# Small triangular inversions on 32x32 tiles of the tensor engine instead of 64x64 ones

## The chip, the cores and the metric

The kernel runs on 1 core of one Trainium2 chip. The metric is the device time of one execution in microseconds (us). The kernel before took 3010.54 us, the median of 3 runs (3006.62 to 3010.95).

## The reference

Three transformer-like blocks run one after the other on 512 tokens of width 1024, all in float32. Two of them hold a recurrence that is computed in chunks, and each chunk needs the inverse of a unit lower triangular matrix:

- the gated delta rule of block 1 (8 heads, chunks of 64 tokens in the reference; the kernel takes 128). Cut to its core:

```
amat = where(strict, kk * decay * beta, 0)          # per head and chunk, strictly lower
t = triangular_solve(eye + amat, rhs, lower=True, unit_diagonal=True)
```

- the RWKV-7 recurrence of block 2 (8 heads), which the reference runs token by token and the kernel in chunks of 64 tokens, again with an inverse of a unit triangular matrix per head and chunk.

Everything else (projections, feed-forward parts, norms, attention with a top-k mask, convolutions) is dense products and elementwise work; the change does not touch it.

## The kernel before

All matrices lie with 128 partitions. Of the projection products ("dense" steps, lines 1063 to 1065) each is three products of a 128x128 weight with a 128x512 operand in a rounded float32 format; they are most of the tensor engine's work.

**The order.** One list gives, for every engine, the order of its steps. In the stages with recurrences the list is made by a planner, `weave`: it takes chains of small dependent steps (one chain per group of heads) and a supply of dense tiles, simulates the engines with a table of costs per step (`SEG`, lines 297 to 312: `p`, `v`, `s`, `g` are the tensor, vector, scalar and GpSimd engines) and writes down the order in which it would issue them. So a changed cost in the table moves steps of all engines. Every engine works strictly through its own list, and steps wait for each other by semaphores. On the tensor engine dense tiles fill the time between small steps.

**The inversions.** There are 12: 8 for the heads of the delta rule (kind `g`, four chunks of 128 tokens each side by side in a 128x512 tile) and 4 for pairs of heads of RWKV-7 (kind `r`, eight chunks of 64 tokens for two heads: two rows of eight 64x64 blocks, in a 128x512 tile). The strictly triangular matrix is first masked to its 16x16 diagonal blocks. Their inverse is the product (I - D)(I + D^2)(I + D^4)(I + D^8), so in three levels the kernel squares D and its transpose (tiles `d` and `e`) and updates the partial product `p`:

- `il` (line 1245), levels 0 and 1: two products, d'e into one bank and e'd into another; level 2: one. The scalar engine copies one bank to `e` (line 2700), the vector engine the other to `d` (line 1955).
- `ip` (line 1257), three levels: e'p into a third bank.
- `ipv` (line 1957), three levels: the vector engine adds that bank to `p`, 128x512 at a time (line 1960).

Then the blocks of 16 are joined to blocks of 32, 64 (and, for kind g, 128) by the steps `it` (transpose of p), `im`, `in_`, `iu` and masked copies made by GpSimd (`iq`).

**How a product is issued.** The products of `il` and `ip`, and those of `im` and `in_`, go through `product(v)`, which is `blocks64` (kind g, lines 1105 to 1112: the 64x64 blocks on the diagonal, 8 matmuls) or `halves64` (kind r, lines 1114 to 1121: 16 matmuls). Each is a float32 matmul of 64 rows by 64 columns with 64 columns moving, on two diagonal 64x64 tiles of the array in turn. A float32 matmul with a small operand stands in the trace as two records of MATMUL and two of LDWEIGHTS. `turned` (line 1128) transposes on the same two tiles, `corner` (line 1237) multiplies 64x64 blocks off the diagonal, and `rt` and `rm` of kind r (transposes and 64x64 products for the recurrence) are woven between the steps of the inversion.

In numbers: each inversion has 5 products in `il` and 3 in `ip`, so 8 products of 16-blocks: 64 for kind g and 32 for kind r.

Of the kernel before, what the change touches and what calls it, by code (L numbers as in the profile page):

```python
# [14 lines left out]
MUL, ADD, SUB, MAX, MIN = ALU.mult, ALU.add, ALU.subtract, ALU.max, ALU.min  # L15
# [148 lines left out]
    return ap.rearrange("p (t i) -> p t i", t=4)  # L164


def v8(ap):
    return ap.rearrange("p (t i) -> p t i", t=8)

# [120 lines left out]
def IXN(qb, h):  # L290
# [7 lines left out]
    dense="p1.36", sums="p.32 v2.0 s.69", xd="p.43 v.68", bt="p.43 s.6", cb="p.86 v.68", st0="v1.7", st="p.86 v1.14",  # L298
    ch="p.23 v.68", che="s2.1", cm="v.75|g1.3", sz="s.6 v.69", sy="p1.6 v1.6", sn1="s.63", sn1p="p.25", sn2="v2.7", sn2p="p.45", sn3="v.74",
    pair="s.63 v.75", hq="p.86", hqs="s1.2", hn="v6.9", hnp="p.43", hn2="s.6", hg="p.23 v1.38 s1.23", hb="p.23 v1.5",  # L300
    eq="p.43 s.6", ek="p.43 s.6", ea="v1.6", eb="v3.2", ec="v1.0", ep="p.43 s.6", hu="p1.72 v1.38", i0="g1.3|p.43 s.6 v1.5", il="p1.0 s.6|v.69", il2="p.5 s.6", iu="p.5 s.6", ip="p.5", ipv="v.69", it="p.5 s.6", iq="g1.28", im="p.5 v.69",
    in_="p.5 v.65", hk="p.5 v2.0", hs1="p.22 v.35", hs2="p.22 s.28", hs3="p.54 v.33", ho="s.36", hon="v4.0",
    hos="p.43", ho2="v.74", hz="s.6 v.69", conv="s.72 v2.24", conv2="s.63 v.75", gate="s.6", branch="v.7", part="v1.4", sh="s.69 v.74", wd="s.63",
    ru="p1.2 s1.37", r1="v2.3 s.63", r1p="p.2", r2="v2.6", r2p="p1.72", r3="v2.3", r3p="p.86", r3b="v1.38", r4="v4.4|s1.9",
    ra="p1.9 s.6 v2.1", ril="p1.9 s.6|v.69", ril2="p.95 s.6", riu="p.95 s.6", rip="p.95", rit="p.95 s.6", rim="p.95 v.69", rin_="p.95 v.65",
    rm="p.95 v.69", rt="p.95 s.6", s1="p.25 s.27", s2="p.13 v.4", s4="p.25 v.2", s3="p.36", ry1a="s.6",
    ry1="p.86 v.69", ry2a="s.62", ry2="p.2", ry2n="v2.6", ry3p="p1.72", ry3="v3.0", rg="s.63", ixp="s.6", ixw="p.05 v.2",
    ixs="p.64 s.5 v.6", ixt="v1.2", ax="s.6", ap="s.6", av="p.43 s.6", an0="p.86", an1="s1.18", an2="v5.2", an2p="p.43",
# [7 lines left out]
def seg(s):  # L316

    kind = s[0]
    if kind == "il" and s[1] == 2:
        kind = "il2"  # L320
    if s[0] in ("il", "ip", "it", "im", "in_", "iu") and s[-2] == "r":
        kind = "r" + kind
    return SEG[kind]
# [11 lines left out]
def opens(name, j):  # L335
# [27 lines left out]
    "ipv": lambda n, *v: [("ip", n) + v],  # L363
    "it": lambda *v: [("ipv", 2) + v], "iq": lambda n, *v: [("im", n - 1) + v if n else ("il", 2) + v],
    "im": lambda n, *v: [("iq", n) + v] * (n < 2) + [("in_", n - 1) + v if n else ("ipv", 2) + v],
# [260 lines left out]
def inversion(v, levels):  # L626
    out = [("i0",) + v]
    for lev in range(3):
        out += [("il", lev) + v, ("ip", lev) + v, ("ipv", lev) + v]
    out += [("iq", 0) + v, ("it",) + v]  # L630
    for n in range(levels):
        out += [("im", n) + v] + ([("iu", n - 1) + v] if n else []) + ([("iq", n + 1) + v] if n + 1 < min(levels, 2) else []) + [("in_", n) + v]
    return out
# [10 lines left out]
def rwkv_pair(p):  # L644
    out = [("ru", p), ("r1", p), ("r1p", p), ("r2", p), ("r2p", p), ("r3", p), ("r3p", p), ("r3b", p), ("r4", p),
           ("ra", p), ("rt", p, 0)]
    v = ("r", p)
    for lev in range(3):
        out += [("il", lev) + v, ("ip", lev) + v, ("ipv", lev) + v] + ([("rt", p, lev + 1)] if lev < 2 else [])
# [247 lines left out]
def build(nc, D, out):  # L897
    with ExitStack() as stack:
# [23 lines left out]
        def t(i):  # L922
            return tile[i]
# [115 lines left out]
        def tensor(e, w):  # L1039
# [83 lines left out]
            def turned(b, x, compact):  # L1123

                for c in range(8):
                    for k in (0, 64) if compact else (64 * (c % 2),):
                        g, s = slice(k, k + 64), slice(c * 64, c * 64 + 64)
                        i = e.matmul(b[g, s], x[g, s], C("ident")[g, g], start=True, stop=True)  # L1128
                return i

            def product(v):
                return halves64 if v[0] == "r" else blocks64

# [111 lines left out]
            def il(lev, *v):  # L1245
                V_ = INV[v]
                w.wait_ge(*IV.dve.at("p0", v) if lev == 0 else IV.dve.at("d", v, lev - 1))
                if lev:
                    w.wait_ge(*IV.act.at("e", v, lev - 1))
                elif v[0] == "r":  # L1250
                    w.wait_ge(*RW.act.at("tok", v[1], 0))
                i = product(v)(bank[V_.bx], t(V_.d), t(V_.e))
                if lev < 2:
                    i = product(v)(bank[V_.bz], t(V_.e), t(V_.d))
                i.then_inc(*IV.pe.up("sq", v, lev))

            def ip(lev, *v):
                V_ = INV[v]
                w.wait_ge(*IV.act.at("e", v, lev))
                w.wait_ge(*(IV.dve.at("p", v, lev - 1) if lev else IV.dve.at("p0", v)))  # L1260
                if lev and v[0] == "r":
                    w.wait_ge(*RW.act.at("tok", v[1], lev))
                product(v)(bank[V_.by], t(V_.e), t(V_.p)).then_inc(*IV.pe.up("p", v, lev))

            def it(*v):
                V_ = INV[v]
                w.wait_ge(*IV.dve.at("p", v, 2))
                turned(bank[V_.bx], t(V_.p), v[0] == "r").then_inc(*IV.pe.up("pt", v))

            def im(n, *v):  # L1270
                V_ = INV[v]
                if n < 2:
                    w.wait_ge(*IV.pool.at("q", v, n))
                w.wait_ge(*(IV.dve.at("m", v, n - 1) if n else IV.dve.at("p", v, 2)))
                i = corner(bank[V_.bz], t(V_.L), t(V_.p), 64) if n == 2 else product(v)(bank[V_.bz], t(V_.d), t(V_.p))
                i.then_inc(*IV.pe.up("y", v, n))

# [358 lines left out]
        def vector(e, w):  # L1636
# [320 lines left out]
            def ipv(lev, *v):  # L1957
                V_ = INV[v]
                w.wait_ge(*IV.pe.at("p", v, lev))
                e.tensor_tensor(t(V_.p), t(V_.p), bank[V_.by], ADD).then_inc(*IV.dve.up("p", v, lev))  # L1960

            def im(n, *v):
                V_ = INV[v]
# [583 lines left out]
            def fc4(h):  # L2547
# [5 lines left out]

            do = dict(acc=acc, rms2=rms2, rms=rms, h=h, xg=xg, xscale=xscale, pair=pair, ffg=ffg, ffs=ffs, ffu=ffu, res=res,
                      conv=conv, conv2=conv2, sums=sums, xd=xd, st0=st0, st=st, ch=ch, cb=cb, cm=cm, sz=sz, sy=sy, sn2=sn2,
                      sn3=sn3, i0=i0, il=il, ipv=ipv, im=im, in_=in_, ea=ea, eb=eb, ec=ec, hn=hn, hg=hg, hb=hb, hu=hu, hk=hk, hs1=hs1, hs3=hs3,
                      hon=hon, ho2=ho2, hz=hz, part=part, branch=branch, ada0=ada0, ada=ada, ada3=ada3, halves=halves,
                      ixw=ixw, ixs=ixs, ixt=ixt, sh=sh, r1=r1, r2=r2, r3=r3, r3b=r3b, r4=r4, ra=ra, rm=rm, s2=s2, s4=s4, ry1=ry1,
                      ry2n=ry2n, ry3=ry3, an2=an2, sa=sa, sb=sb, dg=dg, do_=do_, gv=gv, gw=gw, gn=gn, gnn=gnn, gn2=gn2, gs=gs,
# [656 lines left out]
```

## Time and profile before

| | |
|---|---|
| median of 3 runs | 3010.54 us |
| the profiled execution itself | 3006.34 us |
| its span (first to last instruction) | 3004.6 us |
| tensor engine busy | 2925.2 us, 97% |
| vector engine busy | 1531.4 us, 51% |
| scalar engine busy | 1062.9 us, 35% |
| GpSimd busy | 1375.9 us, 46% |
| mean granted clock of the tensor engine | 0.989 |

A busy tensor engine is one with at least one matmul under way; matmuls overlap in the array, so that the time of one record (218 ns for a 64x64 one) is not what it costs. What a step costs on the chain is the distance from its start to the next one's. The inversions of kind g lie between 265 and 670 us, those of kind r between 1190 and 1245 us and between 1410 and 1465 us.

### The profile page before, as it was taken

The page shows a single profiled execution, that of the slowest core. Times are in us where ns is not written, and L with a number is a line of the kernel's source. Part 1 is how long each engine was busy: PE and PEld are TensorE (multiplying, and loading weights), DVE is VectorE, ACT ScalarE, POOL GpSimd, SP SyncE. Part 2 cuts the span into 40 slices and gives each one's busy share as a digit, 9 for nine tenths or more (in the row PEclk, how much of TensorE's full clock was granted, in tenths as well). Part 3 has the DMA queues.
Part 4 walks back from the last instruction along what each step waited for, and adds up shares of the span by engine and source line. Part 5 has one row for each costly group of instructions (what it writes and reads, how often), then busy time and mean ns, then how long its engine had stood idle before and what let it go on. Part 6 is the DMA issues. An engine that isn't in the chain of part 4 may idle for free.

```text
span 3004.6 us, 45720 instructions
## 1 busy us (share of the span) xinstructions
PE 2925.2 (97%) x18672; PEld 2364.3 (79%) x18672; DVE 1531.4 (51%) x3042; ACT 1062.9 (35%) x1760; POOL 1375.9 (46%) x1781
## 2 busy tenths in 40 slices
PE   6999999999999999999999999999999999999999
PEld 5778888877888887857877788888877778888887
DVE  5776567575666416459543543333375773333310
ACT  4453333333322223233234433222454554332221
POOL 4555334345556553124244365555443334545553
PEclk9999999999999999979999999999999999999999
DMA  3212212112444431102022223333322112233332
GB/s 124 84 57 68 68 56 69 58 49 88 125 148 147 125 101 61 31 30 77 24 67 88 64 85 98 94 94 109 99 77 64 57 57 92 91 94 96 98 104 86
DMA packets 72081, 247.99 MB, mean 83 GB/s; under 512 B 8128, under 2 KB 8512, under 8 KB 71744
## 3 DMA queue, kind: packets, MB, share of 16 engines
q1 hardware_dynamic: 71872, 245.08, 26.6%
q8 instruction: 147, 2.41, 0.3%
q14 instruction: 62, 0.51, 0.1%
HBM read 242.95 MB, written 2.10 MB: 82 GB/s over the span
## 4 chain that ended last, share of the span: by engine, by line
PE 88%; DVE 9%; ACT 2%; issue 1%; POOL 0%; DMA 0%; SPq 0%; DVEq 0%; ACTq 0%
PE bank L1063 25%; PE bank L1065 24%; PE bank L1064 24%; PE bank L1120 2%; PE bank L1111 2%; PE bank L1097 2%; PE bank L1563 1%; PE bank L1074 1%; PE bank L1128 1%; PE bank L1581 1%; PE bank L1404 1%; PE bank L1572 1%; PE bank L1103 1%; DVE sm L1655 0%; DVE t L1716 0%
## 5 line engine op out<-in xcount | busy, mean ns | idle before, releaser
L2981 POOL TENSOR_TENSOR R<-W,R 128x256 fp32r<-128x256 f32 x1715 | 1294.5, 788 | 1511.5 <-ACT R L2573 1511.3
L1063 PE MATMUL bank<-u,R 128*128 128x512 f32 (+1 forms) x3440 | 1389.5, 404 | 14.6 <-DVE t L1784 3.6
L1065 PE MATMUL bank<-u,R 128*128 128x512 f32 (+1 forms) x3440 | 1346.1, 391 | 0.0
L1064 PE MATMUL bank<-u,R 128*128 128x512 f32 (+1 forms) x3440 | 1345.4, 391 | 0.0
L1063 PEld LDWEIGHTS bank<-u,R 128*128 128x128 f32 (+1 forms) x3440 | 648.0, 188 | 166.0 <-issue 12.0
L1065 PEld LDWEIGHTS bank<-u,R 128*128 128x128 f32 (+1 forms) x3440 | 647.2, 188 | 141.4 <-issue 0.6
L1064 PEld LDWEIGHTS bank<-u,R 128*128 128x128 f32 (+1 forms) x3440 | 648.7, 189 | 128.2 <-issue 5.0
L2573 ACT ACTIVATE R<-W 128x1024 fp32r<-128x1024 f32 (+2 forms) x452 | 451.5, 1005 | 141.9 <-PE bank L1065 135.2
L2603 ACT ACTIVATE u<-t 128x512 fp32r<-128x512 f32 x126 | 78.2, 630 | 300.6 <-DVE t L1762 249.2
L1773 DVE SCALAR_TENSOR_TENSOR X<-bank,X 128x512 f32<-128x512 f32 x32 | 22.1, 692 | 239.0 <-PE bank L1065 239.0
L1748 DVE TENSOR_TENSOR t<-bank,t 128x512 f32<-128x512 f32 x66 | 45.5, 689 | 174.3 <-PE bank L1065 164.5
L2610 ACT ACTIVATE t<-t 128x512 f32<-128x512 f32 x66 | 41.7, 632 | 240.4 <-DVE t L1748 240.4
L1740 DVE TENSOR_TENSOR u<-t,u 128x512 fp32r<-128x512 f32 x126 | 98.5, 794 | 55.2 <-ACT u L2603 54.9
L1762 DVE TENSOR_TENSOR t<-t,bank 128x512 f32<-128x512 f32 x66 | 45.4, 687 | 129.1 <-PE bank L1065 127.6
L1784 DVE SCALAR_TENSOR_TENSOR t<-bank,sm,t 128x511 f32<-128x511 f32 (+2 forms) x108 | 80.6, 747 | 21.4 <-ACT t L2619 18.8
L2137 DVE SCALAR_TENSOR_TENSOR t<-t,bank 128x512 f32<-128x512 f32 x48 | 32.9, 685 | 94.0 <-PE bank L1065 93.8
L2597 ACT ACTIVATE u<-X,PC 128x512 fp32r<-128x512 f32 x32 | 23.1, 723 | 149.9 <-DVE X L1773 149.9
L1120 PEld LDWEIGHTS bank<-t,t 64*64 64x64 f32 x2176 | 67.3, 137 | 7.2 <-issue 6.3
L2892 ACT ACTIVATE t<-t,sm 128x128 f32<-128x128 f32 (+3 forms) x96 | 61.9, 647 | 31.1 <-DVE sm L2366 30.8
L1120 PE MATMUL bank<-t,t 64*64 64x64 f32 x2176 | 70.0, 221 | 2.6 <-ACT t L2827 2.3
L1753 DVE SCALAR_TENSOR_TENSOR t<-t,t 128x512 f32<-128x512 f32 x66 | 52.7, 798 | 37.7 <-ACT t L2610 37.7
L1097 PE MATMUL bank<-CN,t 128*128 128x128 f32 x448 | 64.2, 275 | 5.3 <-DVE t L2100 2.9
(401 smaller groups left out, 2746.6 us busy)
## 6 DMA issues: line engine op xcount, KB each, us to landing
W<-in_in SPq DMA_DIRECT2D x48, 512.0 KB, 3.5
W<-in_ff_in SPq DMA_DIRECT2D x44, 512.0 KB, 3.6
W<-in_g_qkv SPq DMA_DIRECT2D x24, 512.0 KB, 3.5
W<-in_ada SPq DMA_DIRECT2D x24, 512.0 KB, 3.5
W<-in_f1g SPq DMA_DIRECT2D x22, 512.0 KB, 3.5
W<-in_f1u SPq DMA_DIRECT2D x22, 512.0 KB, 3.4
W<-in_f2g SPq DMA_DIRECT2D x22, 512.0 KB, 3.5
W<-in_f2u SPq DMA_DIRECT2D x22, 512.0 KB, 3.5
```

What stands on the lines that cost most here:

```text
L1063: e.matmul(b[0:cols, :], wh, hi, start=(k == 0), stop=False)
L1064: e.matmul(b[0:cols, :], wh, lo, start=False, stop=False)
L1065: i = e.matmul(b[0:cols, :], wl, hi, start=False, stop=(k == KT - 1))
L1097: i = e.transpose(b[:, m * 128:m * 128 + 128], x[:, m * 128:m * 128 + 128], C("ident"))
L1111: i = e.matmul(b[g, s], l[g, s], x[g, s], start=True, stop=True)
L1120: i = e.matmul(b[g, s], l[g, s], x[g, s], start=True, stop=True)
L1740: e.tensor_tensor(r(lo[k]), t(src[k]), r(hi[k]).bitcast(F32), SUB).then_inc(*PR.dve.up("lo", tag, k))
L1784: e.scalar_tensor_tensor(out=c[:, s:512], in0=b[:, 0:512 - s], scalar=half(wname, (3 - s) * nt + gj), in1=c[:, s:512], op0=MUL, op1=ADD).t ...
L2573: e.activation(R[q % NH][:, 0:n], W[p % NW][:, 0:n], ACT.Copy).then_inc(*PN.act.up("hi", key))
L2603: e.activation(r(hi[k]), t(src[k]), ACT.Copy).then_inc(*PR.act.up("hi", tag, k))
L2892: e.activation(ex, ex, ACT.Exp, bias=c[:, 0:1], scale=small[q.nw][:, 32 + 2 * qb + m:33 + 2 * qb + m], accum_out=c[:, 1:2]).then_inc(*AT.a ...
L2981: i = e.tensor_tensor(R[q % NH][:, 1024 + a:1024 + b], W[p % NW][:, a:b], R[q % NH][:, a:b].bitcast(F32), SUB)
```

## The change

The products of `il` and `ip` are issued as 32x32 matmuls on the four diagonal tiles of the array. For kind g that is 16 matmuls in place of 8, for kind r 32 in place of 16. The other products stay as they were. What lies in the 64x64 blocks beside the 32x32 diagonal blocks is then not written by these products: the last addition to `p` (level 2) is made on the diagonal blocks alone, in four instructions of 32 partitions, and the rest of the 64x64 blocks of `p` is set to zero by a new step `ipz` of four memsets, after the addition of level 1. The steps `it` and `im` of level 0 wait for `ipz` as well. The planner's costs of these steps are changed.

```
+def square(ap, k, compact, other=False):
+    a = ap[32 * k:32 * k + 32, :]
+    x = (32 * (k % 2) if compact else 32 * k) ^ (32 if other else 0)
+    return a.rearrange("p (t i) -> p t i", t=8 if compact else 4)[:, :, x:x + 32]
...
-    il="p1.0 s.6|v.69", il2="p.5 s.6", ip="p.5", ipv="v.69",
+    il="p.55 s.6|v.69", il2="p.3 s.6", ip="p.3", ipv="v.69", ipv2="v1.3", ipz="v.8",
-    ril="p1.9 s.6|v.69", ril2="p.95 s.6", rip="p.95",
+    ril="p1.0 s.6|v.69", ril2="p.5 s.6", rip="p.5",
...
-    "it": lambda *v: [("ipv", 2) + v],
+    "ipz": lambda *v: [("ipv", 1) + v],
+    "it": lambda *v: [("ipv", 2) + v, ("ipz",) + v],
...
-        out += [("il", lev) + v, ("ip", lev) + v, ("ipv", lev) + v]
+        out += [("il", lev) + v, ("ip", lev) + v, ("ipv", lev) + v] + ([("ipz",) + v] if lev == 1 else [])
...
+            def quarters32(b, l, x, compact):
+                for c in range(8 if compact else 4):
+                    for k in range(4):
+                        a = 64 * c + 32 * (k % 2) if compact else 128 * c + 32 * k
+                        g, s = slice(32 * k, 32 * k + 32), slice(a, a + 32)
+                        i = e.matmul(b[g, s], l[g, s], x[g, s], start=True, stop=True)
+                return i
...
-                i = product(v)(bank[V_.bx], t(V_.d), t(V_.e))
+                i = quarters32(bank[V_.bx], t(V_.d), t(V_.e), v[0] == "r")
                 if lev < 2:
-                    i = product(v)(bank[V_.bz], t(V_.e), t(V_.d))
+                    i = quarters32(bank[V_.bz], t(V_.e), t(V_.d), v[0] == "r")
...
-                product(v)(bank[V_.by], t(V_.e), t(V_.p)).then_inc(*IV.pe.up("p", v, lev))
+                quarters32(bank[V_.by], t(V_.e), t(V_.p), v[0] == "r").then_inc(*IV.pe.up("p", v, lev))
...
             def it(*v):
                 w.wait_ge(*IV.dve.at("p", v, 2))
+                w.wait_ge(*IV.dve.at("clear", v))
...
             def ipv(lev, *v):
-                e.tensor_tensor(t(V_.p), t(V_.p), bank[V_.by], ADD).then_inc(*IV.dve.up("p", v, lev))
+                if lev < 2:
+                    e.tensor_tensor(t(V_.p), t(V_.p), bank[V_.by], ADD).then_inc(*IV.dve.up("p", v, lev))
+                    return
+                for k in range(4):
+                    x, y = (square(a, k, v[0] == "r") for a in (t(V_.p), bank[V_.by]))
+                    e.tensor_tensor(x, x, y, ADD).then_inc(*IV.dve.up("p", v, lev))
+            def ipz(*v):
+                w.wait_ge(*IV.dve.at("p", v, 1))
+                for k in range(4):
+                    e.memset(square(t(V_.p), k, v[0] == "r", True), 0.0).then_inc(*IV.dve.up("clear", v))
```

## Rows read from the trace of the kernel before

**Rows 1.** The page: busy time of each engine; then the shares of the chain.
```profile
PE 2925.2 (97%) x18672; PEld 2364.3 (79%) x18672; DVE 1531.4 (51%) x3042; ACT 1062.9 (35%) x1760; POOL 1375.9 (46%) x1781
...
PE 88%; DVE 9%; ACT 2%; issue 1%; POOL 0%; DMA 0%; SPq 0%; DVEq 0%; ACTq 0%
```

**Rows 2.** Busy time by stretch: stretch, its length, then PE, PEld, DVE, ACT, POOL, clock.
```profile
265.00:670.00 405.00, 397.62 (x3670) 327.98 (x3669) 254.86 (x502) 141.05 (x268) 169.66 (x210) 1.00 0.19 60
1190.00:1245.00 55.00, 55.00 (x1282) 48.39 (x1282) 29.59 (x52) 16.71 (x27) 13.48 (x16) 1.00 0.08 23
1410.00:1465.00 55.00, 51.88 (x1390) 47.88 (x1387) 46.04 (x88) 12.84 (x22) 7.87 (x8) 0.97 0.05 15
```

**Rows 3.** PE's waits, 265 to 670 us: total us, times, longest.
```profile
PE bank L1063 <- DVE t L1784: 3.1, 3, 1.4
PE bank L1097 <- DVE t L2100: 2.9, 2, 2.8
PE bank L1111 <- DVE t L1978: 0.6, 2, 0.3
```

**Rows 4.** The chain in order of time, kind g: start, us, what.
```profile
267.99 0.89 PE bank L1103 x8
268.88 1.08 PE bank L1111 x32
269.96 0.43 PE bank L1063
270.39 0.23 PE bank L1064
...
274.71 0.61 PE bank L1111 x16
...
281.78 1.54 PE bank L1111 x48
```

**Rows 5.** The chain in order of time, kind r.
```profile
1202.08 0.98 PE bank L1074 x8
...
1212.05 2.01 PE bank L1120 x64
...
1229.73 0.93 PE bank L1128 x32
1230.67 3.79 PE bank L1120 x128
```

**Rows 6.** Timeline of PE, three 64x64 tiles at once: start, us, what.
```profile
304.12 0.22 PE L1237 MATMUL bank<-t,t 64*64 64x64 f32 x1
304.13 0.27 PE L1111 MATMUL bank<-t,t 64*64 64x64 f32 x2
304.18 0.22 PE L1237 MATMUL bank<-t,t 64*64 64x64 f32 x1
304.19 0.22 PE L1111 MATMUL bank<-t,t 64*64 64x64 f32 x1
```

**Rows 7.** Timeline of PE: a matmul with one column moving.
```profile
785.87 0.28 PE L1383 MATMUL bank<-CN,t 128*128 128x1 f32 x2
```

**Rows 8.** The chain: from 64x64 tiles to 64x128 tiles.
```profile
1191.38 2.01 PE bank L1120 x64
1193.40 1.06 PE bank L1415 x4
```

**Rows 9.** DVE's instructions by line: ns min/median/max, first and last start.
```profile
L1960 DVE TENSOR_TENSOR t<-t,bank x36: 674/686/689, 275.4 to 1449.3; 128x512 f32<-128x512 f32 x36
...
L1976 DVE TENSOR_SCALAR t<-bank x8: 416/417/417, 306.7 to 665.7; 64x256 f32<-64x256 f32 x8
...
L2214 DVE MEMSET t<- x3: 112/112/112, 1331.7 to 1368.1; 64x64 f32 x3
```

**Rows 10.** DVE's groups by form: xcount, busy us, mean ns.
```profile
L2069 DVE SCALAR_TENSOR_TENSOR t<-bank,sm,t 128x128 f32<-128x128 f32 x24 | 7.8, 347 | 22.7 <-PE bank L1351 22.7
...
L1968 DVE MEMSET t<- 64x256 f32 x8 | 2.2, 272 | 0.9
```

**Rows 11.** DMA queues, 1221 to 1244 us: packets, MB, share of 16 engines.
```profile
q8 instruction: 6, 0.10, 1.8%
```

More of the change, by code:

```diff
@@ L300 @@
     pair="s.63 v.75", hq="p.86", hqs="s1.2", hn="v6.9", hnp="p.43", hn2="s.6", hg="p.23 v1.38 s1.23", hb="p.23 v1.5",
-    eq="p.43 s.6", ek="p.43 s.6", ea="v1.6", eb="v3.2", ec="v1.0", ep="p.43 s.6", hu="p1.72 v1.38", i0="g1.3|p.43 s.6 v1.5", il="p1.0 s.6|v.69", il2="p.5 s.6", iu="p.5 s.6", ip="p.5", ipv="v.69", it="p.5 s.6", iq="g1.28", im="p.5 v.69",
+    eq="p.43 s.6", ek="p.43 s.6", ea="v1.6", eb="v3.2", ec="v1.0", ep="p.43 s.6", hu="p1.72 v1.38", i0="g1.3|p.43 s.6 v1.5", il="p.55 s.6|v.69", il2="p.3 s.6", iu="p.5 s.6", ip="p.3", ipv="v.69", ipv2="v1.3", ipz="v.8", it="p.5 s.6", iq="g1.28", im="p.5 v.69",
     in_="p.5 v.65", hk="p.5 v2.0", hs1="p.22 v.35", hs2="p.22 s.28", hs3="p.54 v.33", ho="s.36", hon="v4.0",
@@ L304 @@
     ru="p1.2 s1.37", r1="v2.3 s.63", r1p="p.2", r2="v2.6", r2p="p1.72", r3="v2.3", r3p="p.86", r3b="v1.38", r4="v4.4|s1.9",
-    ra="p1.9 s.6 v2.1", ril="p1.9 s.6|v.69", ril2="p.95 s.6", riu="p.95 s.6", rip="p.95", rit="p.95 s.6", rim="p.95 v.69", rin_="p.95 v.65",
+    ra="p1.9 s.6 v2.1", ril="p1.0 s.6|v.69", ril2="p.5 s.6", riu="p.95 s.6", rip="p.5", rit="p.95 s.6", rim="p.95 v.69", rin_="p.95 v.65",
     rm="p.95 v.69", rt="p.95 s.6", s1="p.25 s.27", s2="p.13 v.4", s4="p.25 v.2", s3="p.36", ry1a="s.6",
@@ L318, in seg @@
     kind = s[0]
-    if kind == "il" and s[1] == 2:
-        kind = "il2"
+    if kind in ("il", "ipv") and s[1] == 2:
+        kind += "2"
     if s[0] in ("il", "ip", "it", "im", "in_", "iu") and s[-2] == "r":
@@ L362 @@
     "ip": lambda n, *v: [("il", n) + v] + ([("ipv", n - 1) + v] if n else []) + ([("rt", v[1], n)] if v[0] == "r" and n else []),
-    "ipv": lambda n, *v: [("ip", n) + v],
-    "it": lambda *v: [("ipv", 2) + v], "iq": lambda n, *v: [("im", n - 1) + v if n else ("il", 2) + v],
-    "im": lambda n, *v: [("iq", n) + v] * (n < 2) + [("in_", n - 1) + v if n else ("ipv", 2) + v],
+    "ipv": lambda n, *v: [("ip", n) + v], "ipz": lambda *v: [("ipv", 1) + v],
+    "it": lambda *v: [("ipv", 2) + v, ("ipz",) + v], "iq": lambda n, *v: [("im", n - 1) + v if n else ("il", 2) + v],
+    "im": lambda n, *v: [("iq", n) + v] * (n < 2) + [("in_", n - 1) + v if n else ("ipv", 2) + v] + ([] if n else [("ipz",) + v]),
     "in_": lambda n, *v: [("im", n) + v, ("iu", n - 1) + v if n else ("it",) + v],
@@ L648, in rwkv_pair @@
     for lev in range(3):
-        out += [("il", lev) + v, ("ip", lev) + v, ("ipv", lev) + v] + ([("rt", p, lev + 1)] if lev < 2 else [])
+        out += [("il", lev) + v, ("ip", lev) + v, ("ipv", lev) + v] + ([("rt", p, lev + 1)] if lev < 2 else []) + ([("ipz",) + v] if lev == 1 else [])
     out += [("iq", 0) + v, ("it",) + v, ("rm", p, 1), ("im", 0) + v, ("in_", 0) + v, ("rm", p, 2), ("iq", 1) + v, ("iu", 0) + v,
@@ L1274, in im @@
                 w.wait_ge(*(IV.dve.at("m", v, n - 1) if n else IV.dve.at("p", v, 2)))
+                if n == 0:
+                    w.wait_ge(*IV.dve.at("clear", v))
                 i = corner(bank[V_.bz], t(V_.L), t(V_.p), 64) if n == 2 else product(v)(bank[V_.bz], t(V_.d), t(V_.p))
@@ L1959, in ipv @@
                 w.wait_ge(*IV.pe.at("p", v, lev))
-                e.tensor_tensor(t(V_.p), t(V_.p), bank[V_.by], ADD).then_inc(*IV.dve.up("p", v, lev))
+                if lev < 2:
[5 more added lines that the diff above has]
+            def ipz(*v):
+                V_ = INV[v]
+                w.wait_ge(*IV.dve.at("p", v, 1))
+                for k in range(4):
+                    e.memset(square(t(V_.p), k, v[0] == "r", True), 0.0).then_inc(*IV.dve.up("clear", v))
             def im(n, *v):
@@ L2555, in vector @@
                       conv=conv, conv2=conv2, sums=sums, xd=xd, st0=st0, st=st, ch=ch, cb=cb, cm=cm, sz=sz, sy=sy, sn2=sn2,
-                      sn3=sn3, i0=i0, il=il, ipv=ipv, im=im, in_=in_, ea=ea, eb=eb, ec=ec, hn=hn, hg=hg, hb=hb, hu=hu, hk=hk, hs1=hs1, hs3=hs3,
+                      sn3=sn3, i0=i0, il=il, ipv=ipv, ipz=ipz, im=im, in_=in_, ea=ea, eb=eb, ec=ec, hn=hn, hg=hg, hb=hb, hu=hu, hk=hk, hs1=hs1, hs3=hs3,
                       hon=hon, ho2=ho2, hz=hz, part=part, branch=branch, ada0=ada0, ada=ada, ada3=ada3, halves=halves,
```

## The prediction

> **What bounds the kernel now.** I read the page first: the tensor engine (PE) is busy for 97% of the span and holds 88% of the chain that ends last; the vector engine (DVE) is busy for half of it [rows 1]. An average hides stages, so the stretches with inversions come next: PE is busy for 397.6 of 405 us, 55.0 of 55 and 51.9 of 55, DVE for 63%, 54% and 84% [rows 2]. PE's waits say whether small steps hold it up: in the 405 us of kind g it waits 3.1, 2.9 and 0.6 us [rows 3]. So a step of the inversions counts by the time it takes from PE, and the latency of its copies is hidden behind dense tiles, or in kind r behind the other duo's products. The chain in order of time then gives each product's price as distance to the next piece, which a record's own 218 ns does not.
>
> **PE's price of a product, before.** Visits of 16, 32 and 48 records of 64x64 take 0.61, 1.08 and 1.54 us [rows 4]: (1.54 - 0.61)/32 = 0.0291 us a record and 0.145 us for arriving. Kind r agrees: 0.93 for 32 records, 3.79 for 128 [rows 5]. A kind g product (8 matmuls, 16 records) costs 0.466 us, a kind r product (32 records) 0.93. The change touches 64 and 32 of them: 29.8 + 29.8 = 59.6 us of PE, 2048 records.
>
> **What sets 0.0291?** Two tiles work in turn, so each tile takes a record every 0.058 us. On the whole array a 128-column record takes 0.89/8 = 0.111 us [rows 4]. So 64 columns cost 0.053 us and the rest is 0.005 us; by that line a 32-column record costs 0.032 us on its tile. Weight loads follow the same line: records with two moving columns but 128 weight columns still take 0.98/8 = 0.12 us [rows 5], and 32x32 shortens both sides. Is there room for four tiles? Where `corner` (third tile) overlaps `blocks64`, starts on different tiles lie 0.01 us or less apart, three records per 0.06 us [rows 6]; four in 0.032 us are 0.008 apart, just inside that.
>
> **Products after.** Kind g: 32 records on four tiles, 8 rounds of 0.032 = 0.253 us; kind r: 16 rounds, 0.507. Together 64 x 0.253 + 32 x 0.507 = 32.4 us. Gain 27.2 us. Bounds: records that cost columns alone would gain 59.6/2 = 29.8; records that go on costing 0.058 per tile gain nothing (same number of rounds); records that leave one every 0.029 us, whatever their tile, double the time: 59.6 us lost. I take the line through 128 and 64 columns.
>
> **Change of tile shape.** Going from dense to 64x64 costs the 0.145 us above, and the first dense record after takes 0.43 instead of 0.23 [rows 4]. A visit that was isolated pays this before and after. But in the order that the planner writes for the kernel before, I count 42 places (24 in kind g, 18 in kind r) where `il` or `ip` directly adjoins other 64x64 work (`rt`, `rm`, `it`, `im`, ...), free today. No row has 64x64 beside 32x32. The nearest is 64x64 to 64x128: the 64 records before it take 2.01 us [rows 8], as much as 64 records between dense tiles [rows 5] and 0.145 more than 64 x 0.0291; so half a change of shape is as dear as a whole one. 42 x 0.145 = 6.1 us lost; ends 0 and, at 0.2 as after a return to dense, 8.4. I take 6.1. The Trainium skill, TensorEngine Tiling (Array Packing), Key Properties, says that a change of tiling mode, not of tile, drains the engine; by it the 6.1 are due, without it they would be zero, and rows 8 agree for another pair of shapes.
>
> **DVE.** `ipv` at level 2 goes from one 128x512 addition of 0.686 us to four on 32 partitions. Nearest rows: 0.347 for 128 elements per partition (kind g), 0.417 for 256 (kind r) [rows 9, 10]: 1.4 and 1.7 us. `ipz`: memsets of 64 elements cost 0.112, of 256 0.272 [rows 9, 10], so 4 x 0.165 = 0.66 us for kind g and 1.1 for kind r. Extra DVE work: 8 x (1.4 - 0.69 + 0.66) + 4 x (1.7 - 0.69 + 1.1) = 11 + 8.4 = 19.4 us. It lies beside PE's dense tiles. Behind `ipz` in DVE's list stand evacuations of dense banks, for which PE waits two tiles later, and they slip by 0.7 to 1.1 us; PE waits for DVE hardly at all [rows 3], so most of it is slack. The longer `ipv` is made up by shorter products on the same chain (0.21 us on each of five dependent ones in kind g). The new waits of `it` and `im` are for memsets that stand before `ip` level 2 on DVE: nothing. I charge 1 us; 0 and 19.4 (cover gone) are the ends. GpSimd's `iq` and ACT's copies (of `e`) keep their size and start earlier.
>
> **The order.** In kind r some 24 us of PE are 64x64 work without a dense tile, two duos filling each other's gaps. Each duo-level (il 1.87, ip 0.93, rt 0.93) shrinks from 3.7 to 2.4 us, two duos 4.9 us, above the 2 to 3 us of one chain (product, 0.6 us copy, addition). So PE stays the bound, but the planner will put some dense pieces in, each with 0.145 + 0.20 us of arriving and leaving. Six of them: 2 us; ends 0 and 5. Nothing is moved on purpose, yet all later steps are planned anew; I give that no sign. The stretches after 1300 us, where the top-k masks run on DVE, begin earlier and don't shrink.
>
> **Sum.** -27.2 + 6.1 + 1 + 2 = -18 us, against the profiled execution's 3006.3 (span 3004.6): 2988. The median of the runs shown is 4.2 us above that execution; I carry the difference over: 3010.5 - 18 = 2992.5 us.
>
> **Rivals.**
> 1. *The cadence belongs to the engine, not to the tile: slower.* If one record per 0.029 us is what PE's instruction supply yields, 4096 records take 119.2 us: +59.6 + 9 = 3079 us. For: the average never lies below it over a long run [rows 5], and the change needs 8 instructions in 0.032 us. Fetching is a milder form: six packets of instructions in 23 us, 1.8% of 16 engines, so 1.1 us each [rows 11], about 250 instructions; a kind r `il` will eat 256 in 1.0 us. If only kind r is starved to today's pace per record, it loses 30 instead of gaining 13.5: 3010.5 + 30 - 13.7 + 9 = 3036. Against: starts 0.01 us apart on other tiles [rows 6], and dense tiles between visits let the supply get ahead. It decides from a mean of 0.0146 us per record upward, where doubled records cancel halved time. The Trainium skill, TensorE: Matmul & The Clock Gate, "Wait — 56 ns, not 53.3ns?", says that start-to-start never drops below about 25 ns however small the matmul; taken for the whole engine its estimate is 4096 x 0.025 = 102 us, near 3062. Rows 6 contradict it between tiles. Chance 0.09.
> 2. *A small record costs like a 64-column one: about zero.* Then no product is shorter and 9 us are lost: 3020 us; with half of the reduction, 3010.5 - 13.6 + 9 = 3006. Against: with one column moving, the second record of a matmul starts about 0.03 us after the first [rows 7], so 0.032 is not below the floor. The Trainium skill's tiling page, Instruction Overhead, has one column cost what 60 do; with its 60 cycles per pass the estimate is 0.05 us per record, a gain of 8 us and 3011 in all; rows 7 disagree. Chance 0.13.
> 3. *PE gains, but chains give it back.* In the stretch around 1410 us DVE is busy for 84% [rows 2]; if DVE's 19.4 us there and behind evacuations are half exposed, -27.2 + 6.1 + 2 + 10 = -9, 3001.5. Chance 0.10, some of it ending within 0.2%.
>
> **How the numbers follow.** Forecast (a gain of 8 to 28 us) 0.68, rivals 0.09, 0.13, 0.10. Its own range is 2981 to 3003: 27.2 with the low ends of the losses, and a replanned order a few us either way. The range for 8 in 10 reaches into rivals 2 and 3: 2980 to 3012. About 0.2% (6 us) is what a measurement tells from no change. Faster: 0.68 + 0.08 of rival 3 = 0.76. Same: 0.02 + half of rival 2's = 0.10. Slower: 0.09 + the rest = 0.14. That the change doesn't do what it says (32-row tiles side by side) is rivals 1 and 2.
>
> **What would show it.** Chain: an isolated kind g `ip` of 32 records in about 0.145 + 0.25 = 0.40 us (0.61 before), a kind r one in 0.65 (1.08); records on one tile 0.032 apart, four tiles within 0.03. Where 32x32 adjoins 64x64, a gap of some 0.1 us. DVE: four additions of about 0.35 us and four memsets of 0.17. PE's waits for DVE stay at a few us. It is wrong if a 32-record visit takes over 0.6 us (rivals 1, 2), if visits with 64 or more records slow down towards their end (supply), or if PE's waits for DVE grow to tens of us (rival 3).

## The result, and the profile after

The changed kernel takes 3014.89 us (median of 18 runs, 3011.62 to 3019.66) against 3010.32 us of the kernel before on the same chips (18 runs, 3006.62 to 3013.48): ratio 1.0016, 95% interval 1.0010 to 1.0023. It is slower by 3 to 7 us. The forecast was 2992.5 us; the time lies above its range. The profiled execution took 3011.68 us, its span is 3009.9 us.

The products did become shorter. The chain of waits of the kernel after, kind g, in order of time (start, us, what; the answers to [rows 4]; L1144 is the 32x32 product):

```profile
277.13 0.44 PE bank L1104 x4
277.57 0.38 PE bank L1144 x32
...
279.53 0.68 PE bank L1144 x50
```

An isolated `ip` takes 0.38 us; the prediction named 0.40, and 16 records of 64x64 took 0.61 [rows 4]. A pair of products, 64 records, takes 0.68 (the chain's row counts only 50 of them, though the same window holds all 64; the counts in the chains below are low in the same way), so (0.68 - 0.38)/32 = 0.0094 us a record and 0.08 us for arriving.

The same view in kind r, where two duos fill each other's gaps (L1127 is `halves64`, 64x64):

```profile
1238.39 0.55 PE bank L1144 x42
1238.94 1.33 issue
1240.28 0.32 PE bank L1144 x15
1240.60 1.08 PE bank L1127 x32
1241.68 0.82 PE bank L1144 x58
1242.49 1.25 issue
1243.75 0.61 PE bank L1144 x42
```

Here the products are cut in two by `issue`: PE waits for nothing that the profile shows, no semaphore and no engine. The pieces come about every 3.5 us and stand inside a product, between records that wait for nothing. PE's waits, first 1190 to 1480 us, then 265 to 670 us (the answer to [rows 3]):

```profile
PE bank L1144 <- issue: 10.4, 13, 1.5
```

```profile
PE bank L1104 <- DVE t L2046: 4.5, 1, 4.5
PE bank L1104 <- DVE t L1810: 2.4, 1, 2.4
PE bank L1104 <- DVE t L2130: 2.1, 3, 1.7
```

These, the largest waits in the stretch of kind g, are not of the inversions: L1104 is a 128x128 product of the recurrence that follows them (steps `hq` and `hnp`). Only its third had an answer in size in [rows 3]. Stretches of the kernel after (columns as in [rows 2]):

```profile
265.00:670.00 405.00, 392.08 (x4652) 318.01 (x4650) 263.92 (x554) 140.73 (x268) 166.58 (x203) 0.98 0.18 59
1190.00:1245.00 55.00, 51.86 (x1329) 41.10 (x1329) 32.81 (x65) 17.52 (x29) 12.04 (x16) 1.00 0.13 43
1410.00:1465.00 55.00, 49.73 (x1551) 40.67 (x1551) 46.23 (x100) 16.07 (x26) 15.49 (x19) 1.00 0.14 43
610.00:650.00 40.00, 31.82 (x618) 25.80 (x617) 32.11 (x62) 13.17 (x23) 9.59 (x8) 0.83 0.08 22
```

The last row is the place of those waits: 40 us in which PE is busy for 31.8 at a granted clock of 0.83; before it was busy for 39.7 of the same 40 at 1.00. The chain through it (after, start, us, what) shows why:

```profile
612.47 1.78 PE bank L1110 x16
...
629.55 0.70 DVE t L2046
630.30 1.12 PE bank L1104 x4
...
633.93 3.79 PE bank L1110 x16
```

From 619 to 643 us the chain has no dense tile, and most of it is on DVE. In these 24 us PE starts 6 records of dense products, before it started 49. The gates' dense tiles were part of what had filled this place: the last two are taken out of their banks (step `gate`, on the scalar engine) at 573.3 and 580.8 us, before at 616.8 and 624.7. And L1110 x16, which takes 1.78 us in one place of the trace, takes 3.79 in another. Between 620 and 630 us PE had been busy for 3.4 us, and from 623.9 to 637.6 us the granted clock was 0.50, the lower of two levels (1.2 instead of 2.4 GHz). PE is busy for 9.0 us of that stretch, so the clock costs up to 4.5 us there (an estimate: half of the busy time).

DVE's new work by form, kernel after (xcount, busy us, mean ns):

```profile
L1984 DVE TENSOR_TENSOR t<-t,bank 32x128 f32<-32x128 f32 x32 | 9.1, 283 | 4.5 <-PE bank L1144 3.7
L1984 DVE TENSOR_TENSOR t<-t,bank 32x256 f32<-32x256 f32 x16 | 6.7, 417 | 6.7 <-PE bank L1144 6.4
L1990 DVE MEMSET t<- 32x128 f32 x32 | 5.3, 165 | 2.3
L1990 DVE MEMSET t<- 32x256 f32 x16 | 4.4, 272 | 1.4
```

In all 25.5 us in place of 12 x 0.686 = 8.2, so 17.3 us more (19.4 was forecast), and the page's DVE busy time rises from 1531.4 to 1554.5 us; the other 5.8 us of the rise are not in these instructions.

### The profile page after: what moved, and what is told of

The parts are those of the page before. It is cut to its first block, busy times and chain, and to the rows that moved or that the text cites. A ratio compares the mean times of both kernels' runs of the same rounds, so it can differ in the third digit from the quotient of the medians.

```text
span 3009.9 us, 49893 instructions
## 1 busy us (share of the span) xinstructions
PE 2917.1 (97%) x20720; PEld 2348.1 (78%) x20720; DVE 1554.5 (52%) x3126; ACT 1061.9 (35%) x1760; POOL 1377.9 (46%) x1781
## 4 chain that ended last, share of the span: by engine, by line
PE 88%; DVE 9%; ACT 1%; issue 1%; POOL 0%; DMA 0%; SPq 0%; DVEq 0%; ACTq 0%
PE bank L1070 25%; PE bank L1072 24%; PE bank L1071 24%; PE bank L1104 2%; PE bank L1144 1%; PE bank L1127 1%; PE bank L1582 1%; PE bank L1135 1%; PE bank L1081 1%; PE bank L1600 1%; PE bank L1423 1%; PE bank L1591 1%; DVE t L2249 1%; PE bank L1118 1%; PE bank L1110 1%
## 5 line engine op out<-in xcount | busy, mean ns | idle before, releaser
L1104 PE MATMUL bank<-CN,t 128*128 128x128 f32 x448 | 64.8, 277 | 11.3 <-DVE t L2046 4.5
L1104 PEld LDWEIGHTS bank<-CN,t 128*128 128x128 f32 x448 | 52.2, 141 | 26.3 <-DVE t L2046 4.7
L1144 PEld LDWEIGHTS bank<-t,t 32*32 32x32 f32 x4096 | 43.0, 107 | 31.6 <-issue 25.2
```

Source lines behind the costliest of these rows:

```text
L1104: i = e.transpose(b[:, m * 128:m * 128 + 128], x[:, m * 128:m * 128 + 128], C("ident"))
L1144: i = e.matmul(b[g, s], l[g, s], x[g, s], start=True, stop=True)
```

## The experiments

Three suspects stood after this: the supply of instructions to PE (kind r), the planner's new order (kind g), and DVE's extra work. "Old order" below means that the planner is given the costs of before, so that it writes the order of before (two neighbouring steps differ); "new order" that it is given those of after.

Stage lengths from single traces carry some noise: the kernel `e10` below has the instructions and the order of before up to the RWKV stage, yet its delta-rule stage (first dense tile of block 1 to the first of the projection behind it, 25.5 to 695.6 us before) took 677.1 us against 670.1. The granted clock accounts for it. These are the four stretches of that stage with a clock of 0.50 in e10's trace, summed (length, then the busy time of each engine):

```profile
sum 20.60, PE 19.82 PEld 16.72 DVE 14.88 ACT 6.69 POOL 5.87; mean PE 4.95 PEld 4.18 DVE 3.72 ACT 1.67 POOL 1.47
```

In the trace of before PE is busy for 3.2 us at that clock there. The 16.6 us more cost up to 8.3 us (half of them, an estimate), about the 7.0 by which the stages differ. The RWKV/attention stage (1143.4 to 1726.0 us before, and the same dense products in the other traces) repeats better: 582.6 and 582.4 us with the order and the work of before (before and `e3`), 575.9, 575.9 and 576.3 with the new order and the old work (`e10`, `e5` and `e2`). Still, stages only say where to look, and sums are made of ratios. A ratio of 0.1% is 3 us, and most intervals reach 0.1% to either side.

**m1_rates.** PE alone, on copies of the input; nothing of the reference is computed.

```
+ 320 matmuls 32x32 on four tiles in turn; 320 of 64x64 on two; 96 of 32x32 on one tile
+ 12 times: 8 dense matmuls, then 16 of 32x32 on four tiles
```

> A kernel of tensor engine work alone, the rest of the computation left out: 320 float32 matmuls of 32x32 on four diagonal tiles, 320 of 64x64 on two, 96 of 32x32 on one tile, and 12 visits of 16 matmuls of 32x32 between 8 dense ones, each part behind 48 to 60 dense matmuls. Supply theory (instructions come in 16 KB packets of about 256, one per 3.5 us, some of them ahead): the first 32x32 records come every 0.008 us, and after one to two packets' worth the rest comes in bursts with gaps, on average 0.027 us a record; the 64x64 records keep 0.029 throughout. Array theory (the gaps in the changed kernel are data or drains): 32x32 records keep 0.008 to 0.009 us to the end. One tile alone: 0.032 us a record in both. Visits of 32 records: 0.38 us each in both, without gaps.

The chain in order of time (L29 is 32x32 on four tiles, L37 64x64, L43 32x32 on one tile):

```profile
24.45 1.50 PE bank L29 x99
25.95 1.96 issue
27.90 1.27 PE bank L29 x82
29.18 2.18 issue
31.36 1.92 PE bank L29 x96
...
52.36 18.81 PE bank L37 x640
...
82.28 6.92 PE bank L43 x192
```

640 records of 32x32 take 15.3 us, of 64x64 (L37) 18.8, although inside a burst they start 0.008 us apart for the one and 0.029 for the other. The bursts of L29 begin 3.45 us apart, five in all (24.45 to 38.27), 128 records each in the steady state. From the third burst on the granted clock is 0.50, and 128 records take 1.92 us instead of 1.27; the bursts still begin 3.45 us apart. So the array's speed doesn't set this pace. Each record of MATMUL has one of LDWEIGHTS beside it: 256 instructions per 3.45 us, 0.0135 us each. The page's row for the queue gives the size of what arrives:

```profile
q8 instruction: 17, 0.28, 0.8%
```

0.28 MB in 17 packets, 16 KB each, for a program of 4345 instructions: 256 to a packet. In the full kernel 147 packets became 163, and 4173 instructions more are 16.3 packets. The 64x64 records of kind r before the change took 2 x 0.0135 = 0.027 of the 0.029 us that a record lasts: they sat just under the limit. One 32x32 tile by itself (L43) costs 0.032 us a record, as forecast, and four tiles a quarter of it. The mean of the whole run, 6.92/192 = 0.036, mixes two clocks (stretch, length, PE and PEld with the records under way, clock):

```profile
82.50:83.50 1.00, 1.00 (x38) 1.00 (x35) 1.00 0.00 0
87.50:88.50 1.00, 1.00 (x23) 1.00 (x22) 0.50 0.00 0
```

At 1.00 the starts lie 0.032 us apart, at 0.50 0.053. Visits of 32 records between dense tiles (L52) take 0.38 us without a gap, as in kind g.

**e1_old_order.** All of the change's work, with the order of before.

```
-    il="p.55 s.6|v.69", il2="p.3 s.6", ip="p.3", ipv2="v1.3", ipz="v.8", ril="p1.0 s.6|v.69", ril2="p.5 s.6", rip="p.5"
+    il="p1.0 s.6|v.69", il2="p.5 s.6", ip="p.5", ipv2="v.69", ipz="v.01", ril="p1.9 s.6|v.69", ril2="p.95 s.6", rip="p.95"
```

> All of the change's work in the order of the kernel before (the planner's old costs, the new memsets entered as free: the order is that of before but for two steps). Order theory: the delta-rule stage, which ended 8 us late in the changed kernel, ends 6 to 12 us earlier than before; in the stretches of kind r 32x32 products stand back to back without dense tiles, so by the supply theory they gain 0 to 2 us of the 13.6; in all 2999 to 3005. If order does not matter and 32x32 itself is dear: 3013 to 3017, as the changed kernel.

3017.94 us, ratio 1.0028 [1.0018, 1.0037]: both expectations missed, that the old order would bring the gain (2999 to 3005) and, by 1 us, that order doesn't matter (3013 to 3017). In its trace the delta-rule stage is shorter than before (664.3 us against 670.1), the RWKV/attention stage longer (597.9 against 582.6), and PE's waits there (1190 to 1480 us) are:

```profile
PE bank L1144 <- issue: 14.9, 13, 2.5
```

The products stand back to back in that order, and 14.9 us are lost to supply. A second price follows. In the midst of these waits the clock drops, where in the trace of before it is 1.00:

```profile
1220.50:1230.70 10.20, 7.05 (x311) 6.63 (x309) 3.05 (x6) 1.79 (x3) 0.00 (x0) 0.50 0.01 3
```

Over the whole RWKV/attention stage PE is busy at the lower clock for 50.7 us against 39.6 before. That costs up to 5.6 us (half of the difference, an estimate), of the 15.3 by which the stage grew.

**e2_new_order_old_work.** The order of after, with 64x64 products, one whole addition and no memsets.

```
-                i = quarters32(bank[V_.bx], t(V_.d), t(V_.e), v[0] == "r")
+                i = product(v)(bank[V_.bx], t(V_.d), t(V_.e))        # the same in the other two places
-                if lev < 2:
+                if True:                                            # ipv; ipz does nothing
```

> The order of the changed kernel with the work of before: products of 16-blocks as 64x64 matmuls, one addition per level, no memsets. Order theory: slower than the changed kernel, by the 20 us or so that its products are dearer minus the stalls that go: 3020 to 3032, well above before. If the order is harmless: 3008 to 3012, as before.

3014.81 us, ratio 1.0014 [1.0005, 1.0023]: between the two expectations (3020 to 3032, and 3008 to 3012), and slower than before without any new work. PE's waits, 265 to 705 us, have the same lines as after (one line earlier or later in the code), though no product is small:

```profile
PE bank L1105 <- DVE t L2045: 4.3, 1, 4.3
PE bank L1105 <- DVE t L2129: 2.0, 3, 1.7
```

Between 610 and 650 us PE is busy for 32.7 us at a clock of 0.87. So the empty place near 630 us belongs to the order.

**e3_only_g and e4_only_r.** The change for one kind alone, work and planner's costs; the other kind as before.

```
+SMALL_TILES = ("g",)     # e4: ("r",)
+            def first16(v, b, l, x):
+                return quarters32(b, l, x, v[0] == "r") if v[0] in SMALL_TILES else product(v)(b, l, x)
```

> 32x32 products (and new additions, memsets, costs) in the 8 inversions of kind g alone; kind r and its plan as before. The changed kernel's plan for the delta-rule stage is kept, so by the order theory this stage still ends 8 us late: 3016 to 3020. By the theory that kind r carries the loss: 3003 to 3008.

> 32x32 products (and new additions, memsets, costs) in the 4 inversions of kind r alone; kind g and its plan as before. Supply theory: the gaps inside the products (some 12 us in the changed kernel) eat most of the 13.6 us: 3004 to 3009. Theory that kind r carries the loss: 3013 to 3018. Array and drains alone: 2998 to 3001.

Kind g alone: 3015.18 us, 1.0014 [1.0005, 1.0023]. Kind r alone: 3008.63, 0.9996 [0.9987, 1.0005]. Kind r fell in the range of the supply theory; kind g missed its range by 1 us, and its delta-rule stage ended 5 us late (675.2 us against 670.1), not 8. Together +4.2 and -1.2 us are +3.0, near the 4.8 of the whole change: within the noise the kinds act apart.

**e10_r_order_only.** No new work; kind r's costs (and so the order from the RWKV stage on) those of after.

```
 il="p1.0 s.6|v.69", il2="p.5 s.6", ip="p.5"          # kind g: as before
-ril="p1.9 s.6|v.69", ril2="p.95 s.6", rip="p.95"
+ril="p1.0 s.6|v.69", ril2="p.5 s.6", rip="p.5"
```

> No new work anywhere: all products, additions as before; only the planner's costs of kind r's products are those of after (1.0, 0.5, 0.5), and with them the order from the RWKV stage on; up to there the order is that of before. It splits the 11.8 us that the combination of g's work and r's order gained. Theory (r's order alone is worth what the stage showed in e2 and e5, 6 to 7 us, and g's work in before's order the rest, about 5): ratio 0.9975 to 0.9985, 3003 to 3006 us, the RWKV/attention stage 576 us. Rival 1 (all of the gain is the order's, and the new products gain nothing even in kind g): 2998 to 3000. Rival 2 (the gain needs g's work, the order does nothing): 3009 to 3012.

3004.34 us, ratio 0.9980 [0.9971, 0.9989], in the range named; the RWKV/attention stage is 575.9 us against 582.6. The order of after gains 6 us in kind r by itself, and PE's waits from 1190 to 1480 us fall from 9.2 us to 3.8.

**e5_g_work_r_order.** The best parts: kind g's new work in the old order, kind r's new order with the old work.

```
+SMALL_TILES = ("g",)
-    il="p.55 s.6|v.69", il2="p.3 s.6", ip="p.3", ipv2="v1.3", ipz="v.8"
+    il="p1.0 s.6|v.69", il2="p.5 s.6", ip="p.5", ipv2="v.69", ipz="v.01"
```

> Combines what each kind gained in the four kernels so far. Kind g: the new products, additions and memsets, with the planner's costs of before for them, so nearly the order of before in the delta-rule stage. Kind r: the 64x64 products and whole additions of before, with the planner's costs of after (shorter products), so the order of after in the RWKV stages. Theory (order and work act apart in each stage): delta-rule stage 664 us as in e1 (670 before), RWKV/attention stage 576 us as in e2 (583 before), together -12: 2996 to 3002 us, ratio about 0.996. Rival (what the stage gains is lost later or was chance of one trace): within 0.1% of before, 3008 to 3013 us.

2998.47 us (5 runs, 2994.13 to 3003.38), ratio 0.9963 [0.9951, 0.9976]: 11 us faster than before and 16 faster than the change, as expected. The stretches that were holed after are filled again:

```profile
610.00:650.00 40.00, 37.04 (x760) 29.78 (x760) 31.73 (x67) 15.24 (x27) 15.19 (x16) 1.00 0.16 48
1190.00:1245.00 55.00, 55.00 (x1125) 46.77 (x1126) 26.13 (x47) 16.03 (x27) 11.36 (x15) 1.00 0.11 32
```

Its delta-rule stage took 668.7 us, not the 664 of e1 with the same instructions: PE is busy at the lower clock for 13.4 us of it, in e1 for 3.4, which is the noise named above.

**e8_dve_only.** Old order, 64x64 products; only the additions and memsets are new.

```
-            quarters32(...)                                      # e1's il and ip
+            product(v)(...)
                 for k in range(4):                               # ipv, level 2: moved here from ipz
+                    e.memset(square(t(V_.p), k, v[0] == "r", True), 0.0)
                 for k in range(4):
                     e.tensor_tensor(x, x, y, ADD)
```

> The order of before, the 64x64 products of before, but the four additions of the last level and the four memsets (these now just ahead of the additions, so that they don't race with the 64x64 products): the vector engine's extra 19 to 23 us alone. Theory (the vector engine's work is part of where e1's gain went): 2 to 6 us slower than before, of it most in the RWKV/attention stage; the delta-rule stage 671 to 674 us. Rival (it is hidden beside dense tiles, and kind r's loss in e1 is instruction supply alone): within 1.5 us of before, and the RWKV/attention stage 582 to 584 us.

3026.72 us, ratio 1.0054 [1.0042, 1.0067]: 16 us slower, far beyond both expectations. PE's waits of 1190 to 1480 us, and the chain at the longest of them:

```profile
PE bank L1127 <- DVE t L1986: 6.9, 4, 2.5
```

```profile
1248.87 0.27 DVE t L1983
...
1250.32 0.41 DVE t L1986
...
1252.22 2.08 PE bank L1127 x64
```

PE stands from 1248.8 to 1252.2 us. The four memsets and four additions are on the path, 3.3 us where one addition of 0.69 stood. Nearly half of that is this kernel's own, since its memsets come late.

**e11_dve_early_memsets.** The same with the memsets where the change has them; only the `ip` of level 2 (12 of 96 products) is on 32x32 tiles.

> The order of before and all of the vector engine's new work where the full change has it (memsets after the addition of level 1), with only the products of ip at level 2 on 32x32 tiles (12 of 96), all others 64x64. It takes away e8's flaw, that the memsets there stood ahead of the additions and made the chain longer. The 12 small products gain 8 x 0.21 + 4 x 0.42 = 3.4 us by themselves. Theory (the additions and memsets cost time by themselves, instruction supply only matters with all products small): 6 to 12 us slower than before, 3016 to 3022 us, with the waits for the last addition (im, it) in the trace at 4 to 8 us in all. Rival (e8's loss was the place of its memsets): within 2 us of before, 3007 to 3012 us.

3018.41 us, ratio 1.0029 [1.0019, 1.0038]: 8.7 us slower, in the range named. Its small products gain up to 3.4 us and bring 16 changes between 32x32 and 64x64, which cost 1.8 (0.115 each, see below), so DVE's work costs 7 to 10 us in all in the old order. The waits that name the last addition are only 2.3 + 0.9 us:

```profile
PE bank L1135 <- DVE t L1980: 2.5, 1, 2.5
...
PE bank L1127 <- DVE t L1984: 2.3, 2, 1.7
```

below the 4 to 8 us expected. The first row waits for a whole addition of an earlier level (L1980; on DVE it stands behind steps of the top-k masks, and the new memsets some 7 us ahead of it); the corresponding wait was 0.9 us before. The traces place the cost in kind r: the RWKV/attention stage takes 586.0 us against 582.6, with less time at the lower clock (PE busy for 34.1 us against 39.6), while the delta-rule stage, 676.5 us, lies among those with the order and the work of before (670.1 to 677.1). What the rest of the cost is made of these rows don't say.

**m2_bursts.** PE alone again; nothing of the reference is computed.

```
+ 160 matmuls 32x32 on two tiles
+ bursts of 16, 32, 48, 64, 96, 128 matmuls on four tiles, 24 dense ones between
+ four bursts of 64, 6 dense between; then four times 32 matmuls of 64x64, 32 of 32x32
```

> The tensor engine alone. Theory (one packet of 256 instructions per 3.45 us, about one packet ahead): 320 records of 32x32 on two tiles take 8.6 us with idle pieces of about 1 us, not the 5.8 us of array time; bursts of 32, 64, 96 and 128 records after 24 dense matmuls run at 0.009 us a record without idle, and bursts of 192 and 256 records stall once, by 1 to 2 us; four bursts of 128 records with only 6 dense matmuls (1.3 us) between them stall by about 1 us each; alternating visits of 64 records of 64x64 and 64 of 32x32 take 3.45 us a pair, not the 2.7 us of array time and changes of shape. Rival (the pace comes from the engine's queue, not from packets): every burst over some 32 records slows to 0.027 us a record evenly, with no idle pieces.

```profile
24.82 2.71 PE bank L29 x163
27.53 0.72 issue
28.25 2.30 PE bank L29 x128
30.54 1.71 issue
...
72.08 1.37 PE bank L29 x91
73.45 0.41 issue
...
80.15 1.70 PE bank L29 x111
81.85 2.60 issue
...
114.34 2.01 PE bank L37 x64
...
117.87 2.01 PE bank L37 x64
```

On two tiles, 320 records take 8.4 us; with starts 0.016 us apart inside a burst the array would need 5.1. A burst of 64 matmuls (128 records) after dense work has no gap, one of 96 (192 records) stalls for 0.41, one of 128 (256 records) for 2.60 us, where 1 to 2 us had been expected for both. So PE has one to one and a half packets ahead after dense work (326 instructions before the first gap of m1, 374 in the last burst here), then one per 3.45 us. Alternating 64 records of 64x64 and 64 of 32x32, 256 instructions, take 3.45 to 3.73 us a pair (114.34, 117.87, 121.32, 125.05): about the packet's time, as expected, not the 2.7 us of the first pair. The bursts are at full pace until they stop dead: the rival, a queue that slows evenly, is out.

**e9_r_two_tiles_at_a_time.** As e1, but each kind r product visits tiles 0 and 1 for all columns, then 2 and 3.

```
-                for c in range(8):
-                    for k in range(4):
+                for h, c in [(h, c) for h in range(2) for c in range(8)]:
+                    for k in (2 * h, 2 * h + 1):
```

> As e1 (all of after's work in before's order), but each kind r product visits two of the four tiles at a time, first tiles 0 and 1 for all columns, then 2 and 3: the same instructions, twice the array time per product (0.036/2 = 0.018 us a record in place of 0.009). Theory (instruction supply sets kind r's pace, 0.027 us a record over a long run): the same as e1 within 3 us, about 3018 us, and the RWKV/attention stage 596 to 602 us. Rival (the four tiles' array time sets it): 32 products x 32 records x 0.009 = 9 us more, about 3027 us, the stage near 607 us.

3023.35 us, ratio 1.0044 [1.0030, 1.0057]: about 5 us above e1, between what the theory (0 to 3) and the rival (9) gave, so not decisive as a time. (By m1 and m2 a record costs 0.016 us on two tiles, not the 0.018 that the expectation took from a mean over two clocks.) In the trace the waits for supply fall from 14.9 to 6.4 us, as they must if a slower product hides them. From the first `il` of the first two pairs to their last `in_` (about 1200 to 1260 us; 50.4 us before) the 57.9 us of e1 became 59.4, where array time alone would add 4.6; the second two pairs grew by 3.6, at a granted clock of 0.83 in 1430 to 1480 us against 0.90 in e1. Over the RWKV/attention stage (604.3 us against 597.9) PE is busy at the lower clock for 67.4 us against 50.7, which costs up to 8.3 us (half of the difference, an estimate), more than the stage grew. By this estimate the slower products cost nothing beyond the clock, as supply would have it; why the clock was lower no run separates.

## Why the prediction was wrong

The four combinations of order and work, for each kind, in us against the kernel before. Each ratio is turned into us at 3010; the entries marked * are differences of two kernels (kind g: e5 - e10 and e2 - e10; kind r: e1 less kind g's -5), and good to about 4 us.

| | new work, old order | old work, new order | both |
|---|---|---|---|
| kind g | -5 * | +10 * | +4.2 (e3) |
| kind r | +13.5 * | -6.0 (e10) | -1.2 (e4) |

So of the change, kind g's order costs 10 and its work gains 5 to 6; kind r's order gains 6 and its work costs 5. The sum is +3, the whole change +4.8 (3 to 7). The forecast of -18 failed at three of its steps: room on PE for four tiles (taken as free, 10.4 us of waits for instructions in the kernel after), DVE's work (charged 1 us, cost 7 to 10) and the order (given no sign, +10 in kind g and -6 in kind r).

- **What bounds the kernel:** right for the kernel before. "PE waits for DVE hardly at all" was read from the order and the work of before and taken as a property of the stage. In the new order it fails near 630 us, and in the old one more work on DVE cost 7 to 10 us (e11).
- **Price of a product, -27.2 us:** right for the array. 0.38 and 0.68 us for visits of 32 and 64 records, 0.008 to 0.009 us a record over four tiles, 0.032 on one. In kind g 64 x 0.213 = 13.6 us, less 2.8 for 24 changes of shape, are -10.8; -5 was measured. No run splits off the 6 us between; DVE's work is the likely part, though in e11's trace PE waits for the last addition in this stage for only 0.9 us. The Trainium skill, TensorE: Matmul & The Clock Gate, "Wait — 56ns, not 53.3ns?", has no start-to-start below about 25 ns; 0.008 us a record across tiles contradicts it for the engine as a whole, and 0.032 us on one tile (m1) doesn't.
- **"Is there room for four tiles?"** This is the first step that failed. It was answered from starts 0.01 us apart in a handful of records [rows 6], which shows the array's pace over four records, not the supply over 256. The rows that mattered were quoted only under rival 1: 128 records in 3.79 us [rows 5] and a packet every 3.8 us [rows 11] are one packet of 256 instructions for 256 instructions, so the kernel before already drew them nearly as fast as they can come (one packet per 3.45 us by m1). The mild form of rival 1 was therefore the right mechanism, with the wrong price: kind r starved to the old pace would lose 30 us. It gets 0.027 us a record while the store is empty and full pace while it is not; the order of after puts dense pieces between the products, and the loss there stays at 10.4 us. In the old order, without these, it is 14.9, and up to 5.6 more through the clock.
- **Changes of shape, +6.1 us:** fits nearly. 42 were counted, e1's trace (the order of before) has 43 between 32x32 and 64x64, and after's 46. The first record behind one starts 0.148 us after the last 64x64 record or 0.120 after the last 32x32 one, where 0.029 and 0.008 are the mean without a change: some 0.115 us each, 5 us in all. The Trainium skill, TensorEngine Tiling (Array Packing), Key Properties, says that a change of tiling mode drains the engine; for 64x64 beside 32x32 the trace agrees.
- **DVE, +1 us:** the second step that failed, by its size. The instructions were priced nearly right (0.283 and 0.417 us for additions, where 0.347 and 0.417 were forecast; 0.165 and 0.272 for memsets), the cover was not: 7 to 10 us in the old order (e11). The additions lie on the inversion's own chain: `it` and `im` wait for the fourth of them, and in kind r PE stands meanwhile (e8, e11). "Made up by shorter products" would need PE to reach the next product sooner; in kind r supply forbids it.
- **New dense breaks in kind r, +2 us:** wrong in sign. Six were counted, and from 1000 us on e10's trace has 48 changes from 128x128 to 64x64 where before's has 43. With the old work the new order gains 6.0 us (e10), since 5.4 us of waits for small steps are then gone (9.2 before, 3.8 in e10).
- **The order, "no sign":** the third step; in kind g alone it costs 10 us, as much as supply in kind r. The planner was told that products are shorter and DVE's steps longer (which of the two moved the steps, no run separates). It drew dense tiles earlier, the gates' last ones 44 us earlier, and near 630 us small steps of a recurrence stood alone with DVE. The granted clock adds to the loss there, up to 4.5 us in after's trace.
- **Rival 3** (DVE's new work is half exposed, 10 us, around 1410 us and behind evacuations) has the price of DVE's work nearly, and its place: kind r, by e11. It did not see the place near 630 us. The rivals' 0.32 of chance held two of the three mechanisms; none of them held the planner's order, nor the total.
- **Sums:** the chances of the recorded text are off by 0.015. "Same" is 0.02 + 0.065 = 0.085 and not 0.10, "slower" then 0.155 and not 0.14.

Against the forecast of -18: products in the array -27; changes of shape +5; supply +10; DVE beyond cover +7 to +10, if it costs in the new order what it does in the old; kind g's order +10; kind r's order -6. That is -1 to +2, where 4.8 (3 to 7) was measured. Terms that are differences of ratios are good to some 4 us, and the 3 to 6 us that are left are not assigned.

## What to carry to other kernels

Halving a small operation's array time is worth little once its instructions arrive slower than they run: count instructions per us of the stretch (here 0.0135 us each, one packet of 256 per 3.45 us) before counting columns. When a planner or scheduler reads a cost table, a changed cost is a change of its own; time it with the old work, and the work with the old order, before judging either. The combination that the four quarters pointed to gained 11 us, where the change as written lost 5.

## What the runs showed of the hardware

- Instructions reach the engine in packets of 16 KB, 256 instructions, on a queue of their own (m1: 17 packets for 4345 instructions). When PE takes them faster, one comes per 3.45 us (m1, at a granted clock of 1.00 and of 0.50), and PE stands idle between the bursts with nothing in the profile but `issue`.
- After dense work it holds one to one and a half packets: 256 instructions run through at full pace, 384 lose 0.4 us, 512 lose 2.6 us (m2).
- At a granted clock of 1.00 a 32x32 float32 record costs 0.032 us on one tile, 0.016 on two and 0.008 over four (m1, m2), a 64x64 one 0.029 over two tiles. At 0.50 the 32x32 one costs 0.053 on one tile and 0.013 over four (m1).
- Four additions on 32 partitions and 256 elements take 4 x 0.42 = 1.7 us, and one on 128 partitions and 512 elements 0.69, though the four hold half as many elements. One on 32 partitions and 128 elements takes 0.283, a copy of 128 partitions and 128 elements 0.286 (after's trace): the elements per partition set the time of these, not the partitions.
- Where supply or DVE holds PE up, the granted clock can drop from 1.00 to 0.50 for some us behind it: in e1 from 1220.5 to 1230.7 us, in after from 623.9 to 637.6 us (PE busy for 3.4 us of 620 to 630). The same 16 records of L1110 took 1.78 and 3.79 us in after's trace.
